# A two-layer hybrid decoder trunk: the gate product moved to GpSimd, a modulation pair and top-k rounds moved, one convolution tap given to ScalarE

## The reference

```python
mod = (c_act @ w_mod[l] + b_mod[l])[:, None, :]
sh1, sc1, g1, sh2, sc2, g2 = jnp.split(mod, 6, axis=-1)
h = x * (1.0 + sc1) + sh1
q, k, v, qi, ki, wi, xr, yg = jnp.split(h @ w_in[l], split_at, axis=-1)
# q, k, qi, ki are turned by rotary tables
attn_out = dsa_attention(q, k, v, qi, ki, wi)     # 4 heads; an indexer of 8 heads picks the top 128 keys of each query
xc = causal_depthwise_conv(xr, conv_w[l], conv_b[l])    # 4 taps
# rg_lru: r, i = sigmoid(blockdiag(xc)); a = exp(-8 r softplus(-lam))
#         u = sqrt(1 - a^2) * (i * xc);  h_t = a_t h_{t-1} + u_t
lru_out = rg_lru(xc, ...) * jax.nn.gelu(yg, approximate=True)
merged = concat([rms_norm(attn_out, g_attn), rms_norm(lru_out, g_lru)])
x = layer_norm(alpha * x + (1.0 + g1) * (merged @ w_out[l]), ln1_g[l], ln1_b[l])
h2 = x * (1.0 + sc2) + sh2
x = layer_norm(alpha * x + (1.0 + g2) * (square(relu(h2 @ w_up[l])) @ w_down[l]), ln2_g[l], ln2_b[l])
```

## Time and profile before

| what | value |
|---|---|
| median of 3 runs | 1333.34 us |
| the profiled execution's own time | 1331.25 us |
| its span | 1329.3 us |
| PE busy, instructions | 1274.9 us (96%), 6241 |
| VectorE busy | 788.5 us (59%), 1274 |
| ScalarE busy | 551.4 us (41%), 834 |
| GpSimd busy | 152.4 us (11%), 123 |

### The profile page before, as it was taken

How to read it: one execution, slowest core, us unless ns; L and a number is a source line. 1 busy time by engine, 2 the same in 40 slices (tenths; PEclk the granted TensorE clock), 3 DMA queues, 4 the chain that set the end, 5 groups by cost and what they waited for, 6 DMA issues and landing times.

```text
span 1329.3 us, 17078 instructions
## 1 busy us (share of the span) xinstructions
PE 1274.9 (96%) x6241; PEld 1001.6 (75%) x6241; DVE 788.5 (59%) x1274; ACT 551.4 (41%) x834; POOL 152.4 (11%) x123
## 2 busy tenths in 40 slices
PE   4999998999999999999999999789999999999996
PEld 3766766788788888888876676567878888888886
DVE  2748978757734635437475797875674353433354
ACT  2753466534623313314256445662373141332331
POOL 2100343111000000000120023510200000000012
PEclk9999999999999999999999999999999999999997
DMA  9843534321343343342254344511133333233311
GB/s 313 272 155 127 163 132 150 112 80 47 111 159 94 102 156 98 114 143 83 79 176 159 127 136 131 189 53 48 48 104 103 96 94 103 86 110 95 95 64 63
DMA packets 76470, 158.56 MB, mean 119 GB/s; under 512 B 6529, under 2 KB 14969, under 8 KB 76409
## 3 DMA queue, kind: packets, MB, share of 16 engines
q1 hardware_dynamic: 64064, 112.80, 27.2%
q0 software_dynamic: 11712, 44.57, 10.1%
q10 hardware_dynamic: 632, 0.39, 0.1%
HBM read 155.64 MB, written 2.10 MB: 119 GB/s over the span
## 4 chain that ended last, share of the span: by engine, by line
PE 83%; DVE 7%; ACT 5%; issue 2%; DMA 2%; POOL 0%; POOLq 0%; ACTq 0%; SPq 0%; DVEq 0%
PE bank L650 25%; PE bank L652 24%; PE bank L651 24%; PE bank L615 2%; PE bank L697 2%; DMA mod_raw<-in_w_mod_dram 1%; DMA first_mod<-in_w_mod_dram 1%; PE bank L847 1%; PE bank L549 1%; DVE w_lo L1487 1%; DVE resid L1496 1%; DVE a_lo L1529 1%; DVE resid L1491 1%; ACT w_hi L1003 1%; ACT a_hi L1014 1%
## 5 line engine op out<-in xcount | busy, mean ns | idle before, releaser
L1487 DVE TENSOR_TENSOR w_lo<-w_raw,w_hi 128x1024 fp32r<-128x1024 f32 x168 | 206.1, 1233 | 331.2 <-ACT w_hi L1003 331.1
L1003 ACT ACTIVATE w_hi<-w_raw 128x1024 fp32r<-128x1024 f32 x192 | 201.6, 1057 | 446.5 <-PE bank L652 442.4
L650 PE MATMUL bank<-a_hi,w_hi 128*128 128x512 f32 x896 | 360.1, 402 | 3.8 <-DVE w_lo L1487 3.2
L652 PE MATMUL bank<-a_hi,w_lo 128*128 128x512 f32 x896 | 350.2, 391 | 0.0
L651 PE MATMUL bank<-a_lo,w_hi 128*128 128x512 f32 x896 | 349.8, 390 | 0.0
L650 PEld LDWEIGHTS bank<-a_hi,w_hi 128*128 128x128 f32 x896 | 168.5, 188 | 62.9 <-issue 27.2
L650 PE MATMUL bank<-b_hi,w_hi 128*128 128x512 f32 x512 | 199.7, 390 | 0.0
L652 PE MATMUL bank<-b_hi,w_lo 128*128 128x512 f32 x512 | 199.3, 389 | 0.0
L651 PE MATMUL bank<-b_lo,w_hi 128*128 128x512 f32 x512 | 199.2, 389 | 0.0
L652 PEld LDWEIGHTS bank<-a_hi,w_lo 128*128 128x128 f32 x896 | 168.5, 188 | 36.4
L651 PEld LDWEIGHTS bank<-a_lo,w_hi 128*128 128x128 f32 x896 | 168.7, 188 | 35.0 <-issue 1.9
(11 more groups left out here) (256 smaller groups left out, 1409.9 us busy)
## 6 DMA issues: line engine op xcount, KB each, us to landing
mod_raw<-in_w_mod_dram POOLq DMA_DIRECT2D x40, 1024.0 KB, 5.9
w_raw<-in_w_up_dram SPq DMA_DIRECT2D x64, 512.0 KB, 3.7
w_raw<-in_w_down_dram SPq DMA_DIRECT2D x64, 512.0 KB, 3.7
w_raw<-in_w_in_dram SPq DMA_DIRECT2D x48, 512.0 KB, 3.6
first_mod<-in_w_mod_dram SPq DMA_DIRECT2D x8, 1024.0 KB, 13.4
w_raw<-in_w_out_dram SPq DMA_DIRECT2D x16, 512.0 KB, 3.7
x_in<-in_x_dram POOLq DMA_DIRECT2D x4, 512.0 KB, 10.4
out_dram<-y_out SPq DMA_DIRECT2D x8, 256.0 KB, 2.1
```

What stands on the lines that cost most here:

```text
L650: mm(o, wh, hi(kk), start=first, stop=False)
L652: last = mm(o, wl, hi(kk), start=False, stop=fin)
L1003: last = af(hi, src, ACT.Copy)
L1487: last = tt(lo, src, hi.bitcast(F32), ALU.subtract)
```

## The change

- `LN_FILL` goes from 14 to 10.
- The product of input gate and convolution moves from VectorE (inside the units) to GpSimd: tiles 0 to 2 after the low part of yg pair 1, tile 3 after that of yg pair 3. `lru_scan` waits for it.
- Pair 0 of out0 gets its low part after the transfer of modulation pair 12 instead of 11. The last low part of out0 no longer waits for the recurrent output; its turn is given by VectorE at u == 12.
- `late_mod(l, 13)` moves from u == 1 to u == 6.
- ScalarE's `xr_out` writes bias plus the last tap into `xc` from the same bank before it copies `xr`; VectorE's `conv` has three passes left, all of them adding.
- ScalarE scales the residual two tiles at a time after each of the last four `a_tile`s instead of all eight at the end.
- VectorE's rounds of top-k: 34 instead of 26 before the rotation of k, 40 instead of 36 before that of q, 44 instead of 40 before `lru_input(2)`, and all 48 before the units instead of 45.

```diff
-LN_FILL = 14
+LN_FILL = 10
@@ GpSimd
+                def gated(m):
+                    pool.wait_ge(free_s[5], uses_before(5, f"gi{m}", l) + 1)
+                    pool.wait_ge(conv_done, l * LT + (m + 1))
+                    gp.tensor_tensor(xc[:, m, :], xc[:, m, :], gi[:, m, :], ALU.mult).then_inc(lru_gated, 1)
-                lows_after = {7: lows[0:1], 8: lows[1:3], 9: lows[3:5], 10: lows[5:7], 11: lows[7:9], 12: lows[9:11]}
+                lows_after = {7: lows[0:1], 8: lows[1:3], 9: lows[3:5], 10: lows[5:7], 11: lows[7:8], 12: lows[8:11]}
...
                         low_part(name, p)
+                        if (name, p) == lows[5]:
+                            for m in range(LT - 1):
+                                gated(m)
+                        if (name, p) == lows[7]:
+                            gated(LT - 1)
...
                     if n == LATE_PAIRS - 2:
-                        pool.wait_ge(lru_out, l * LT + LT)
                         low_part(*lows[11])
@@ PE
-                    if u == 1:
+                    if u == 6:
                         late_mod(l, 13)
@@ ScalarE
                         act.wait_ge(full_s[m], uses_before(m, f"xr{m}", l) + 1)
+                        af(xc[:, m, :], banks[m][:, :], ACT.Identity, bias=vcol("conv_b", m),
+                           scale=vcol("conv_w", (CONV - 1) * LT + m))
                         af(xr[:, m, CONV - 1:], banks[m][:, :], ACT.Copy).then_inc(free_s[m], 1)
...
-                scale_residual(1)
+                    if kk >= DK // 2:
+                        scale_residual(1, range(2 * kk - DK, 2 * kk - DK + 2))
@@ VectorE
-                    for j in range(CONV):
-                        w = vcol("conv_w", j * LT + m)
-                        src = xr[:, m, j:j + T]
-                        if j == 0:
-                            step(ts(xc[:, m, :], src, w, vcol("conv_b", m), ALU.mult, ALU.add))
+                    for j in range(CONV - 1):
+                        if j:
+                            step.settle()
+                        ins = stt(xc[:, m, :], xr[:, m, j:j + T], vcol("conv_w", j * LT + m), xc[:, m, :], ALU.mult, ALU.add)
...
-                topk(26)
+                ve.sem_inc(lo_turn, 1)
+                topk(34)
                 k_out()
-                for p, rounds_ in enumerate((29, 32, 34, 36)):
+                for rounds_ in (37, 40):
                     ve.sem_inc(lo_turn, 1)
                     topk(rounds_)
                 q_out()
                 ve.sem_inc(lo_turn, 1)
-                topk(39)
+                topk(43)
                 lru_input(0)
                 lru_input(1)
-                topk(40)
+                topk(44)
                 lru_input(2)
                 lru_input(3)
-                for rounds_ in (42, 44, 45):
+                for rounds_ in (46, 47, 48):
                     ve.sem_inc(lo_turn, 1)
                     topk(rounds_)
...
-                    topk(min(45 + u + 1, 3 * per))
-                    if 1 <= u < 1 + LT:
-                        lru_gated(u - 1)
+                    if u == 12:
+                        ve.sem_inc(lo_turn, 1)
```

More of the change, by code:

```diff
@@ L303, in trunk_kernel @@
         attn_sq, root_diag_s = sem("attn_squared"), sem("root_roots_ready")
-        lru_squared = sem("decay_squared")
+        lru_squared, lru_gated = sem("decay_squared"), sem("lru_input_gated")
         pv_done = sem("pv_done")
@@ L1700, in conv @@
                     ve.wait_ge(free_s[m], uses_before(m, f"xr{m}", l) + 1)
-                    for j in range(CONV):
-                        w = vcol("conv_w", j * LT + m)
-                        src = xr[:, m, j:j + T]
-                        if j == 0:
-                            step(ts(xc[:, m, :], src, w, vcol("conv_b", m), ALU.mult, ALU.add))
-                        else:
[L1707 to L1712, removed]
+                    for j in range(CONV - 1):
+                        if j:
+                            step.settle()
+                        ins = stt(xc[:, m, :], xr[:, m, j:j + T], vcol("conv_w", j * LT + m), xc[:, m, :], ALU.mult, ALU.add)
+                        if j == CONV - 2:
+                            ins.then_inc(conv_done, 1)
+                        else:
+                            step(ins)
                 split_lo("v", l, 0)
@@ L1741, in layer @@
                     topk(rounds_)
[L1743 to L1747, removed]
                 def lru_input(m):
@@ L1758, in lru_scan @@
                     ve.wait_ge(lru_sqrt, l * LT + (m + 1))
+                    ve.wait_ge(lru_gated, l * LT + (m + 1))
                     step(tt(th[:, m, :], th[:, m, :], xc[:, m, :], ALU.mult))
```

## The result

The changed kernel takes 1317.44 us (median of 4 runs, 1316.02 to 1318.94), the kernel before 1333.76 us beside it; the ratio is 0.9881, 95% interval 0.9861 to 0.9900. Forecast were 1317 us and a range of 1311 to 1324. The profiled execution took 1316.02 us, its span 1314.4 us, 14.9 us less than before.

What follows compares the result with a forecast made beforehand. PE, 83% of the last-ending chain, bounds the kernel, so its waits and low clock offer time. Attention -16.1, norms -1.4, clock +0.6, copy +0.8 give -16.1 on 1331.25: 1315.2, plus 2.1 to the median: 1317 us, range 1311 to 1324.

Steps and rivals of the forecast that it cites:

- first norm, layers 0 and 1: First norm of each layer: fewer identity matmuls, up1's 1.6 us wait gone, a new 1.3 us wait; gain 0.5 us each.
- norm between the layers: Third norm: fewer identity matmuls let PE start earlier, but its second low part comes just late; gain 0.4 us.
- allowance for the clock: Norms: the clock can fall in the 0.4 us gaps that the fillers leave; cost 0.6 us.
- xr copy, layer 1: ScalarE's new instruction in layer 1 makes the second and fourth banks 0.55 and 0.25 us late; cost 0.8 us.
- Item 1: Attention: moving pair 13 to u = 6 removes transfer waits of 4.1 and 6.5 us, leaving 0.5 and 1.2 us.
- Item 2: Attention, behind the wait for pair 13: the low clock goes, giving 1.4 us in layer 0 and 1.8 in layer 1.
- Item 3: Attention units: less VectorE work cuts PE's waits for exponentials; gain 2.0 us per layer, bounds 0 and 3.
- Rival A: Attention: only the waits for the transfer go, VectorE's relief shows nothing; gain 9.9 us, time 1323.4 us, chance 0.19.
- The last low part at nothing: Attention: out0's last low part waits for u = 12; pair 15 still lands in time, cost nothing, bound 2 us per layer.
- VectorE 1 us early at the row maxima: Ahead of the attention: one top-k round fewer behind q, so VectorE reaches the row maxima about 1 us earlier; cost nothing.
- The meetings with GpSimd: Groups q and yg: GpSimd's products meet VectorE's top-k, cost nothing; if they met rotations, up to 4.8 us per layer.
- Rival C: Attention: PE loses its clock in short matmuls with gaps; whole gain gone, or 9 us slower at 1342; chance 0.04.

Runs made afterwards that it cites:

- low part after gelu: Changed kernel with GpSimd's last low part of out0 waiting again for the recurrent output (fourth gelu product): 1315.9 us.
- product on VectorE: Changed kernel with the product of input gate and convolution back on VectorE, in units 1 to 4: 1318.4 us.
- norms as before: Changed kernel with 14 matmuls on the identity again and the residual scaled in one piece after the eighth tile: 1318.6 us.
- one scaling per tile: Changed kernel with one residual tile scaled after each of activation tiles 4 to 6 and the other five after tile 7: 1314.8 us.
- pair 13 back: Changed kernel with modulation pair 13 used at u = 1 again instead of u = 6: 1334.1 us.
- pair 13 first: Changed kernel with pair 13's transfer issued ahead of the low part of out0's pair 2 on GpSimd, not behind it: 1315.2 us.
- rounds back: Changed kernel with the top-k rounds spread as before the change, three rounds and the last mask inside units 0 to 2: 1320.0 us.
- three edits: Changed kernel with out0's last low part behind the fourth gelu product, pair 13's transfer ahead of pair 2's low part, and residual scaling spread singly: 1309.8 us.

## Why the prediction was right

The time and the main mechanism held: the move of pair 13 with the low clock behind it, and VectorE's relief. That the median came within half a microsecond of 1317 is luck. The span of the profiled execution fell by 14.9 us and not by 16.1, and errors of 1 to 2 us of either sign lie within that. By its terms, in the profiled execution:

| term | forecast | measured |
|---|---|---|
| attention, layer 0 | -7.0 | -6.45 |
| attention, layer 1 | -9.1 | -9.4 |
| first norm, layers 0 and 1 | -0.5, -0.5 | -0.85, -1.55 |
| norm between the layers | -0.4 | +1.7 |
| allowance for the clock | +0.6 | in the two rows above |
| xr copy, layer 1 | +0.8 | +0.6 |
| start of the kernel | 0 | +2.1 |
| all else | 0 | -1.1 |
| span | -16.1 | -14.9 |

Each is a difference of two stretches between the same instructions. The first norm of layer 1 has in it 1.05 us of low clock that the kernel before had. The copy is read from pair 3's products to the next indexer matmuls: 3.17 us after, 2.57 before. Of the last row 0.8 us lie behind down0 of layer 1, where the granted clock of the last 38 us was 0.86 instead of 0.81.

- *Item 1, the transfer.* Its wait fell to 1.2 us in both layers; forecast were 0.5 and 1.2. PE reached pair 13 5.2 us after the first transpose (forecast 5.6, though the parts that it names, 8.5 less 1.3 less 1.0, give 6.2). The prediction had not looked at what stands ahead of this transfer on GpSimd: the low part that the change puts there fills it until 218.7, some 0.7 us behind PE's release of the buffer, going by the kernel in which the issue comes first. The other half of the wait is a slower transfer, 7.8 and 7.7 us against 6.2 in layer 0 of the kernel before. The reason that the prediction gave, SyncE's loads, stays open. A load starts 0.2 us behind the issue in the changed kernel; in the kernel before none did in layer 0, and in layer 1, where the transfer took 9.0 us, one started 1.3 us ahead of it. The edit that took the wait away moved that load too.
- *Item 2, the clock.* No stretch at the low level in the changed kernel's attention, as forecast.
- *Item 3, VectorE's relief.* Sized 2.0 us per layer, bounds 0 and 3. Between the kernel with only pair 13 moved and the changed one lie 3.0 and 2.9 us (in layer 1 with some low clock in the former), although the changed one pays 1.2 us of transfer and 0.84 us of stand that the other doesn't have. The term was too small, and two costs that were put at nothing or at less (0.84 at unit 13, 0.7 more at pair 13 in layer 0) made up for it.
- *Rival A*, that the gain is the transfer's alone, is wrong for the change as a whole: 9.1 of the 16.3 us come without the relief. The kernel with only pair 13 moved took 1323.7 us and A said 1323.4, but that is luck as well. A's sum has 1.0 us for the clock where item 2 has 3.2; with item 2's figure it is 12.1 us, 1321. And A had no new waits, where waits of 1 to 1.7 us for exponentials took the transfer's place.
- *The last low part at nothing.* This step failed. Pair 15 was in time, as forecast (issue 239.77, no wait at its use). But the turn at u == 12 let GpSimd start beside the fourth gelu product, which the wait on the recurrent output had kept apart. The prediction asked only for the transfer behind the low part, not whom it meets. By the trace 0.84 us in each layer.
- *VectorE 1 us early at the row maxima.* Wrong: it had no idle time before them. It lost 1.1 us in the mask beside GpSimd. PE hardly felt it: 0.32 and 0.33 us before the first transpose, 0.21 and 0.51 before.
- *The meetings with GpSimd.* The rule of the Trainium skill that the prediction used (SBUF — State Buffer, section "SBUF: two separate sides") agrees with the late gelu product, which reads two inputs (2.53 us). For the mask, which reads one, the same section of the Trainium skill has VectorE's two-port performance modes among what GpSimd excludes; that the mask runs in one is not shown here. The products themselves met nothing: GpSimd took 1.28 us for each (forecast 1.2). A rotation step of k took 2.86 us beside the low part of yg's pair 0, a meeting that the prediction had counted as even.
- *The norms.* 0.5 us each at full clock was near; the 0.93 us wait for the eighth tile (forecast 1.3) and the end of the 1.6 us wait came as described. The prediction's 72 matmuls ahead of that wait are 75 in the trace; its 332.7 is the sum with 75, so the slip is in the text alone. Rival C stayed away in the attention, but the clock fell in the norm between the layers (0.57, ten matmuls in 3.76 instead of 2.56 us): against the same stretch at full clock in the kernel with the low part after gelu, 2.25 us. The kernel before had a fall of its own in layer 1's first norm, 1.05 us, which the changed one hadn't. So the prediction's "only a stand of 4 us or more was followed by the low one" held for the attention that it looked at, and not for the trace as a whole: here PE worked without a gap.

```profile
953.00:957.00 4.00, 4.00 (x14) 2.86 (x15) 2.35 (x8) 0.20 (x1) 0.00 (x0) 0.57 0.01 4
```

- *The start.* The second modulation pair landed later in the profiled execution (below). No edit touches that part. But of the kernel before there is one trace, so whether its early landing is chance isn't shown.

## What to carry to other kernels

When a wait goes, the gain is bounded by what else was hidden beneath it: here 10 us of transfer and clock came at once, but 5.8 us more only because VectorE's work had left the same units, and with the transfer's wait left in place everything else in the change was worth nothing in the sum. Of every step that is moved to GpSimd or gets a new turn, ask two things: what transfer now queues behind it, and which instruction of VectorE it meets (here products of two inputs and a mask were held up, MAX8 was not). A semaphore that is set when the data is done kept the gelu product and the low part apart; a turn given by the sequencer didn't.

## What the runs showed of the hardware

- *A turn runs ahead.* In VectorE's program the turn at u == 12 stands behind the fourth gelu product, a sum of squares and the next row maximum. GpSimd was released at 237.46, while VectorE was still in the row maximum of unit 12 (237.25 to 237.93), before any of the three had begun. The Trainium skill (Perfetto Trace Analysis, section "Sequencer Loop") fits: engine instructions are pushed into a queue, and a control instruction is started by the sequencer when it is read.
- *A short stand can be followed by the low level, or not.* After 2.21 us of waiting for pair 13 PE ran at 0.50 for some 3 us (product on VectorE, layer 0); after 2.33 us (norms as before, layer 1) and 2.04 us (one scaling per tile, layer 0) at 1.00. After waits of 0.98 and 1.69 us in two units running it ran at 0.50 for some 3 us in layer 1 of the kernel with only pair 13 moved, and at 1.00 after the same two waits in layer 0.
- *The fall in a norm wanders.* It was in layer 1's first norm in the kernel before and with only pair 13 moved; between the layers in the changed kernel, with pair 13 back and with the norms as before; in layer 0's with pair 13 first (ten matmuls in 3.73 us at 309.87); in layers 0 and 1 with the rounds back. The other five kernels had none in that execution. It comes with 14 matmuls on the identity and with 10. It cost 1.05 and 2.25 us where it was read, and hides any smaller gain in a norm unless the stretch is read at equal clock.
- *The first transfer.* PE's wait for the second modulation pair at the start was 4.36 us in the one trace of the kernel before and 6.0 to 7.4 us in the eleven others (6.44 in the changed kernel, 6.63 with only pair 13 moved, 7.20 with the three edits): up to 3 us of span in a part that no edit touches.
